# Attention's second pass: three score banks throughout, an out bank of its own for the third pair of heads, and the first merge weights' low part by GpSimd

## The reference, cut to what matters

```python
def nsa_mixer(...):
    ...
    sc = einsum('bghqd,bgcd->bghqc', qb, kc) * scale - slopes * dist_c      # 31 compressed keys
    pc = masked_softmax(sc, dist_c >= 0)
    o_cmp = einsum('bghqc,bgcd->bghqd', pc, vc)
    ...
    ss = einsum('bghqd,bgqkd->bghqk', qb, k_g) * scale - slopes * dist_s    # selected blocks
    o_slc = einsum('bghqk,bgqkd->bghqd', masked_softmax(ss, dist_s >= 0), v_g)
    ...
    sw = einsum('bghqd,bgkd->bghqk', qb, kwb) * scale - slopes * dist_w     # window
    o_win = einsum('bghqk,bgkd->bghqd', masked_softmax(sw, mask_w), vwb)
    return gb[..., 0:1] * o_cmp + gb[..., 1:2] * o_slc + gb[..., 2:3] * o_win

def s5_mixer(...):
    ...
    yg = gelu(y)
    return yg * sigmoid(yg @ w_glu + b_glu)

def first_block(...):
    ...
    merged = gate[..., 0, :] * (y_ssm @ w_proj_ssm) + gate[..., 1, :] * (y_nsa @ w_proj_nsa)
    x = x + merged @ w_out
    ...
```

## Time and profile before

| what | value |
|---|---|
| time, median of 3 runs | 1800.06 us (1797.25 to 1800.57) |
| the profiled execution's own time | 1799.23 us |
| its span, first to last instruction | 1797.5 us |
| mean granted TensorE clock | 0.975 |
| PE busy | 1710.7 us (95%), 7645 matmuls |
| PEld busy | 1307.8 us (73%) |
| DVE busy | 1187.4 us (66%) |
| ACT busy | 730.1 us (41%) |
| POOL busy | 465.7 us (26%) |
| HBM traffic | 90 GB/s over the span |

### The profile page before, as it was taken

One profiled execution on the slowest core, in us unless ns is written; L12 is line 12 of the kernel. 1 busy time (PEld: TensorE's weight loads), 2 busy tenths in 40 slices (PEclk: granted clock), 3 DMA queues, 4 the chain that ended last, 5 costly groups with the idle time before them and its releaser, 6 DMA issues.

```text
span 1797.5 us, 21556 instructions
## 1 busy us (share of the span) xinstructions
PE 1710.7 (95%) x7645; PEld 1307.8 (73%) x7645; DVE 1187.4 (66%) x2193; ACT 730.1 (41%) x1176; POOL 465.7 (26%) x448
## 2 busy tenths in 40 slices
PE   7998898899997999999999999999999899999997
PEld 4456654578885888888876887978757588888885
DVE  5976654344446675577556457988884687877786
ACT  3164455533244331133125437566461443333234
POOL 2832200020020110011000114232330266556552
PEclk9999789999998999999999999999999899999999
DMA  6245110043332454455431122121311332423311
GB/s 152 73 98 139 34 60 1 18 118 98 104 130 91 166 176 140 141 186 176 140 117 48 48 59 65 42 59 48 106 47 47 117 117 72 139 71 103 108 42 53
DMA packets 185537, 168.69 MB, mean 94 GB/s; under 512 B 17639, under 2 KB 168867, under 8 KB 185051
## 3 DMA queue, kind: packets, MB, share of 16 engines
q1 hardware_dynamic: 173083, 128.19, 23.4%
q0 software_dynamic: 11808, 39.29, 7.4%
q10 hardware_dynamic: 560, 0.12, 0.0%
HBM read 155.83 MB, written 6.31 MB: 90 GB/s over the span
## 4 chain that ended last, share of the span: by engine, by line
PE 77%; DVE 10%; ACT 7%; issue 3%; DMA 2%; POOL 1%; SPq 0%; DVEq 0%; ACTq 0%; POOLq 0%
PE bank L1508 28%; PE bank L1925 18%; PE bank L1619 3%; PE bank L1813 3%; DVE arena L2680 2%; PE bank L1668 2%; PE bank L1461 2%; PE bank L1447 2%; PE bank L1301 2%; PE bank L1624 2%; PE bank L1403 1%; PE bank L1805 1%; DMA ring<-in_w_in 1%; PE bank L1727 1%; PE bank L1659 1%
## 5 line engine op out<-in xcount | busy, mean ns | idle before, releaser
L3595 DVE SCALAR_TENSOR_TENSOR arena<-bank,ffn_taps,arena 128x441 f32<-128x441 f32 (+2 forms) x352 | 221.3, 689 | 75.7 <-ACT arena L2638 75.4
L3051 DVE TENSOR_TENSOR w_lo<-ring,w_hi 128x2048 fp32r<-128x2048 f32 x52 | 119.2, 2292 | 117.0 <-ACT w_hi L2212 113.2
L1508 PE MATMUL bank<-h_lo,w_hi 128*128 128x512 f32 x448 | 176.5, 394 | 3.2 <-DVE w_lo L3051 1.8
L2212 ACT CAST w_hi<-ring 128x2048 fp32r<-128x2048 f32 x52 | 99.1, 1907 | 176.4 <-PE bank L1508 176.4
L1508 PE MATMUL bank<-hT_hi,w_hi 128*128 128x512 f32 x384 | 153.5, 400 | 6.6 <-DVE h_lo L3137 5.9
L1157 POOL TENSOR_TENSOR w_lo<-ring,w_hi 128x2048 fp32r<-128x2048 f32 x21 | 99.6, 4742 | 165.1 <-ACT w_hi L2611 165.1
L1508 PE MATMUL bank<-act_hi,w_hi 128*128 128x512 f32 x352 | 137.9, 392 | 0.2
L1508 PE MATMUL bank<-act_lo,w_hi 128*128 128x512 f32 x352 | 131.8, 389 | 0.0
L1925 PE MATMUL bank<-hT_hi,w_hi 128*128 128x512 f32 x336 | 130.8, 389 | 0.3 <-POOL w_lo L1157 0.3
L1925 PE MATMUL bank<-hT_hi,w_lo 128*128 128x512 f32 x336 | 130.7, 389 | 0.0
L1925 PE MATMUL bank<-h_lo,w_hi 128*128 128x512 f32 x336 | 130.7, 389 | 0.0
(11 more groups left out here) (578 smaller groups left out, 4020.4 us busy)
## 6 DMA issues: line engine op xcount, KB each, us to landing
ring<-in_w_up SPq DMA_DIRECT2D x76, 512.0 KB, 4.5
arena<-in_w_mod POOLq DMA_DIRECT2D x48, 512.0 KB, 4.2
ring<-in_w_in SPq DMA_DIRECT2D x72, 256.0 KB, 3.1
ring<-in_w_down SPq DMA_DIRECT2D x32, 512.0 KB, 4.1
ring<-in_w_in SPq DMA_DIRECT2D x30, 512.0 KB, 4.0
arena<-in_w_down SPq DMA_DIRECT2D x22, 512.0 KB, 4.3
ring<-in_w_out SPq DMA_DIRECT2D x8, 512.0 KB, 3.9
ring<-in_w_out SPq DMA_DIRECT2D x16, 256.0 KB, 3.0
```

The lines of the kernel that those rows point to most:

```text
L1508: ins = pe.matmul(out, u[:, n % SLOTS, cols], v[:, k, :], start=start and k == w[0][0] and m == 0, stop=stop and k == w[-1][0] and m == 2)
L2212: sc.copy(w_hi[:, n % SLOTS, :], ring[:, n % SLOTS, :]).then_inc(hi_ready, 1)
L3051: ve.tensor_tensor(w_lo[:, n % SLOTS, :], ring[:, n % SLOTS, :], value(w_hi[:, n % SLOTS, :]), ALU.subtract)\
L3595: return ve.scalar_tensor_tensor(o[:, ys, xs], x[:, yt, xt], ffn_taps[:, at:at + 1], o[:, ys, xs], ALU.mult, ALU.add)
```

## The change

Five edits belong together.

1. `part_bank` gives all items the banks 0, 1 and 2 in turn, and a score waits for the item three before it, from the first item on.
2. The third pair of heads accumulates in bank 5; the others stay in bank 3. So TensorE waits for the out bank only at the second pair (for the first pair's read) and at the fourth (for the second pair's read, no longer the third's). The first `glu` tile, which writes bank 5, waits for the third pair's read.
3. In ScalarE's and VectorE's lists the high and low part of the second and third pair's outputs move from the start of the items 36 and 54 behind the scores of the items 39 and 40, and of 57 and 58. The first pair's stay where they were.
4. The fourth `glu` tile goes to bank 4 instead of bank 2, and the wait for its sigmoid ahead of the merge's second product goes.
5. The first merge chunk's `w_lo` is subtracted by GpSimd, as soon as ScalarE's cast is done, and VectorE's `low` for it goes; a wait for it is put before VectorE's next `low`.

```diff
         def part_bank(s):
-            return banks[s % 2 if s < ITEMS // KVG else (0, 1, 4)[s % 3]]
-
-        glu_banks = banks[5], banks[6], banks[7], banks[2]
+            return banks[s % 3]
+
+        def out_bank(c):
+
+            return banks[5 if c == 2 else 3]
+
+        glu_banks = banks[5], banks[6], banks[7], banks[4]
...
             pool.dma_start(yT, y_scr.rearrange("(m p) s j -> p m s j", p=P)).then_inc(y_in, 16)
 
+            n = C0["merge"] % SLOTS
+            pool.wait_ge(hi_ready, 1)
+            pool.tensor_tensor(w_lo[:, n, :], ring[:, n, :], value(w_hi[:, n, :]), ALU.subtract).then_inc(split_ready, 1)
+
             pool.wait_ge(merged_ready, 2)
...
                 if s % (HPG * PARTS) == 0:
                     pe.wait_ge(row_done, h + HPG)
-                if s >= 2:
-                    pe.wait_ge(part_ready, s - 1 if s < ITEMS // KVG + 2 else s - 2)
+                if s >= 3:
+                    pe.wait_ge(part_ready, s - 2)
...
                 h, j, m, b = part_of(s)
-                if s % (2 * PARTS) == 0 and s:
-                    pe.wait_ge(o_out, s // (2 * PARTS))
+                c = s // (2 * PARTS)
+                if s % (2 * PARTS) == 0 and c in (1, 3):
+                    pe.wait_ge(o_out, 1 if c == 1 else 2)
                 pe.wait_ge(part_ready, s + 1)
-                o = banks[3]
+                o = out_bank(c)
...
                     arrived(n)
                     pe.wait_ge(gelu_done, UT)
+                    pe.wait_ge(o_out, 3)
...
                         t = T0["merge"] + 2 * m + j
-                        if (m, j) == (0, 1):
-                            pe.wait_ge(glu_sig, UT)
                         claim(t, i)
...
                 sc.wait_ge(pv_done, 2 * PARTS * (c + 1))
-                sc.copy(nsa_hi[:, c, :], banks[3][:]).then_inc(nsa_hi_ready, 1)
+                sc.copy(nsa_hi[:, c, :], out_bank(c)[:]).then_inc(nsa_hi_ready, 1)
...
             for s in range(ITEMS):
-                if s % (2 * PARTS) == 0 and s:
-                    nsa_high(s // (2 * PARTS) - 1)
+                if s == 2 * PARTS:
+                    nsa_high(0)
                 if s + AHEAD < ITEMS:
                     part(s + AHEAD)
+                if s in (4 * PARTS + 1, 6 * PARTS + 1):
+                    nsa_high(s // (2 * PARTS) - 1)
...
                 ve.wait_ge(nsa_hi_ready, c + 1)
-                ve.tensor_tensor(nsa_lo[:, c, :], banks[3][:], value(nsa_hi[:, c, :]), ALU.subtract).then_inc(o_out, 1)
+                ve.tensor_tensor(nsa_lo[:, c, :], out_bank(c)[:], value(nsa_hi[:, c, :]), ALU.subtract).then_inc(o_out, 1)
...
             for s in range(ITEMS):
-                if s % (2 * PARTS) == 0 and s:
-                    nsa_low(s // (2 * PARTS) - 1)
+                if s == 2 * PARTS:
+                    nsa_low(0)
...
                     part_mask(s + AHEAD)
+                if s in (4 * PARTS + 2, 6 * PARTS + 2):
+                    nsa_low(s // (2 * PARTS) - 1)
...
             free(ve, chunk_used)
-            low(C0["merge"], 0)
             nsa_low(HEADS // 2 - 1)
...
                 product(y_ssm[:, m, :], gelu_y[:, m, :], yT[:, m].rearrange("p s j -> p (s j)")).then_inc(yssm_ready, 1)
+            ve.wait_ge(split_ready, 1)
             low(C0["merge"] + 1, 1)
```

## The result

The changed kernel takes 1789.27 us (median of 6 executions, 1785.46 to 1791.69), the kernel before 1799.30 in the same series (1797.12 to 1800.57): ratio 0.9944, 95% interval 0.9929 to 0.9959. That is 10.0 us where 5.2 to 5.7 were forecast (1794.4, from 1799.6 or 1800.06); the time lies under the range. Two later series give ratios of 0.9952 and 0.9957; over all three the mean of 17 executions is 1789.8, that of 79 executions of the kernel before 1798.6, so 8.8 us (95% about +-1.4).

The account below looks back on a forecast made before the run. TensorE's matmuls were taken as a floor, so only its waits could go: 0.75 + 1.15 + 1.78 + 1.52 = 5.2 us. From 1799.23 us that gave 1794.0, moved half way to the median: 1794.4, range 1791.2 to 1798.2.

Parts of the forecast that it names:

- Three banks: Scores of item 33 finish inside the wait for exponentials, so the values of item 31 start earlier: 0.75 us gained.
- Third pair: At item 36, values start 1.61 us earlier, but the moved high part delays the gelus: 1.15 us gained.
- Fourth pair: At item 54, values start at 336.42 instead of 338.20 us, with no gelus behind: 1.78 us gained.
- Merge: Merge starts 1.95 us earlier, but its second chunk newly waits 0.43 us for w_lo: 1.52 us gained.
- Load and GpSimd: Third chunk's earlier load and GpSimd's subtraction of the first w_lo, covered by 4.4 to 6.8 us: cost 0 each.
- Sum: All gains over the second pass and the merge's start together: 5.2 us.
- I take the same cost: Low clock behind the gelu pause, 2.9 us lost before, costs the same though the pause grows to about 4.6 us.
- that the clock isn't cut at the gelu pause: Rival: no low clock behind the gelu pause, so 2.9 us come back as well: 1791.5 us, chance 10%.
- the others: Rivals: clock low longer, 1797.3 us, 15%; gain given back by ScalarE and load, 1796.7, 19%; long low clock before glu, 1807.4, 6%.

Follow-up runs that it names:

- banks and GpSimd alone: Two runs: the changed kernel with the first w_lo back on VectorE, 1792.76 us; the kernel before with only GpSimd subtracting that w_lo, 1796.83 us.
- the late read: The changed kernel with the third pair's high and low part moved behind the gelus in ScalarE's and VectorE's lists: 1791.98 us, ratio 0.9955.
- the filled changed kernel: The changed kernel plus useless matmuls in seven TensorE pauses of over 2 us behind 300 us: 1786.02 us (0.9925), in a later series 1783.46 (0.9919).

## Why the prediction was wrong

Its terms, against the profile. *Three banks*, 0.75: the values of 31 start at 296.40, the pass itself at 235.93 instead of 237.84; 298.94 - 296.40 - 1.91 = 0.63, for 0.75. *Third pair*, 1.15: 317.70 became 314.03, 3.67 less, of which 1.91 and 0.63 were there already: 1.13, with the moved high part in it, as predicted. *Fourth pair*, 1.78: the earlier trace rows 338.20 became 332.18, 6.02; the 2.35 beyond the 3.67 are 1.61 of pause and its start-up, and 0.6 from the low stretch behind the gelus, in which TensorE had 4.7 us of work, not 5.8. *Merge*, 1.52: 372.35 became 364.17, and the second chunk waits 0.40 for 0.43 forecast; it starts at 373.02, not 380.66, so 1.62 more than the 6.02. *Load and GpSimd*, 0 each: the cast ended in time; the 4.51 us were covered. *Sum*, 5.2: 5.6 to 6.0 in the stretch that holds the change, in three profiles against two, 0.6 of it by the clock behind the gelus and not by a wait; banks and GpSimd alone gave 4.3 and 0.8 of it. *Start*: the forecast went out from 1799.6, and the mean of 79 executions is 1798.6. This is 1.0 of the 4.6 us between the forecast, 1794.4, and the mean of 17, 1789.8; the other 3.6 are what the measured 8.8 has over 5.2, 2.7 of it the clock's by the mean of all executions.

**The step that failed** is the clock's: "I take the same cost". It priced one pause, the gelus', whose cost really changed by only 0.6 us, and put low clock everywhere else at no change, without a reason. In its place the runs showed: less low clock behind the changed part. In the kernel before, two of two profiles have both the stretch at 576 and the one at 1044; of the changed kernel's three, two have neither and one has one. In these five the stretch from 506 to 1187 us is 1.6 to 5.2 us shorter, against a term of 0; with the three profiles that have matmuls added behind the merge it is 2.3 in the mean; by the mean clock of all executions it is 2.7 over the whole span. The range, 1791.2 at its low end, had room for one stretch of 2.9 us, but not for this together with the 1.0 of the start.

The Trainium skill, "TensorE: Matmul & The Clock Gate", Part 1, was read in the prediction as a rule about one pause. It says that the same kernel shows more or fewer slow matmuls from run to run. The traces agree: two profiles of the kernel before have their low stretches at the same places within 0.7 us, but the two with matmuls added, which run the same program up to 501 us, have 3.4 us behind the gelus, not 6.8, and 3.4 at the merge's start; and of the changed kernel's three, one has 3.4 us more at 929 us and one at 1038 that the others lack. What the sentence does not say is that the mean clock over executions still differs between the two kernels, by 0.0014, or the 2.7 us above. Averaging over executions narrows the noise, but does not take this away.

The rivals: that the clock isn't cut at the gelu pause did not come (0.50 from 311.9 to 318.7), though its number, 1791.5, lay nearer; the others erred to the slow side.

Open: why a given pause is followed by low clock in one kernel and not in another, which these runs do not tell; whether the changed kernel's advantage in low clock would outlive an unrelated edit elsewhere. The run with two matmuls added kept its ratio (0.9947), though its profile has a third stretch of 679.3 us; the late read did so in part (0.9955).

## What to carry to other kernels

Sum the removed waits from the timeline, and check the sum in a stretch between two pauses that both kernels have; here that was right within 0.4 to 0.8 us. Before work is added as a test, look whether a wait behind it takes it in: here 1.33 us of it vanished so. Then give the clock a width of its own: list the low stretches of the trace everywhere behind the edit, not just beside it, and half of their work is what may come or go. Compare the mean granted clock of all executions of both kernels, not of one profile each. Useless matmuls in the long pauses gained 8.1 us in the kernel before, more than this change's waits, and 8.0 in the changed one in the one series that has both (2.6 from one series to another, 1788.57 to 1786.02).

## What the hardware showed

- Filling one pause alone gained nothing (0.9946); its one profile has low stretches at 571 and 1035 us which two of the changed kernel's three profiles lack. Filling seven did gain (0.9925 and 0.9919). That the low clock moves on to the next pause that is left is not shown.
- Pauses of 1.0 us (ahead of 1044), 1.8 (369), 2.7 (574) and 4.1 us (314) were each followed by 3.2 to 6.9 us at about 0.50. The one at 369 was so in two of five unfilled profiles, and the one of 2.7 us not in the changed kernel's three.
- A low stretch isn't always lost time. In the filled changed kernel, at full clock, 549 to 556 us has TensorE busy 5.32 of 7.00 us, since there it waits for VectorE's `h_lo`. This may be a part of why filling the kernel before gained 8.1 us and not the 14 that half of the work would make:

```profile
549.00:556.00 7.00, 5.32 (x17) 2.91 (x18) 7.00 (x13) 3.12 (x6) 0.00 (x0) 1.00 0.00 0
```

- One stretch at 0.50, at 1029 to 1044 us, has no pause ahead of it but a wait of 1.0 us for ScalarE's `early_hi`, in filled kernels too (1.03 us, and 3.2 us at 0.50 from 1029.1). No run here says what brings it.
- The span from the start to 231 to 237 us varies by up to 6.5 us (230.67 to 237.22) between kernels that are equal up to there; two profiles should not be compared by their spans before that is taken off.
